# The second tile's attention beside the expert gathers: one step for each part, and the probabilities scaled by VectorE

## What is computed

```python
h = rms_norm(x, mix_norm[i])
q, c_kv, iq, ik, iw, q_mem = jnp.split(h @ a_w_in[j], A_SPLITS, axis=-1)
# dsa_attention, for a block of 128 queries
_, sel = lax.top_k(score, topk)
logits = jnp.einsum('bqhc,bqkc->bhqk', q_lat, c_sel) * (A_HEAD_DIM ** -0.5) + bias
p = jax.nn.softmax(logits, axis=-1)
# memory_attention
logits = jnp.einsum('bqhd,bmhd->bhqm', q, k) * (MEM_HEAD_DIM ** -0.5)
p = jax.nn.softmax(logits, axis=-1)
x = x + jnp.concatenate([seq_out, mem_out], axis=-1) @ w_o[i]
# peer_ffn: 8 retrieval heads of 16 experts = 128 rows of u and of v for each token
act = jax.nn.gelu(jnp.einsum('td,thkd->thk', xt, u[et]))
out = jnp.einsum('thk,thkd->td', act * gt, v[et])
```

## Time and profile before

| | before |
|---|---|
| median of 3 runs | 3037.27 us (3035.47 to 3040.38) |
| profiled execution | 3040.9 us, its span 3039.1 us |
| busy share of the span | PE 82%, DVE 47%, ACT 30%, POOL 23% |
| mean granted TensorE clock | 0.934 of full speed |
| DMA | 1105.17 MB moved, mean 364 GB/s |
| chain that ended last | DMA 43%, PE 40%, DVE 9%, issue 4%, ACT 4% |

### The profile page before, as it was taken

One profiled execution on the slowest core, in us unless ns is written; L12 is line 12 of the kernel. 1 busy time (PEld: TensorE's weight loads), 2 busy tenths in 40 slices (PEclk: granted clock), 3 DMA queues, 4 the chain that ended last, 5 costly groups with the idle time before them and its releaser, 6 DMA issues.

```text
span 3039.1 us, 33538 instructions
## 1 busy us (share of the span) xinstructions
PE 2490.9 (82%) x11846; PEld 1339.6 (44%) x11846; DVE 1422.4 (47%) x3358; ACT 900.5 (30%) x2366; POOL 694.1 (23%) x626
## 2 busy tenths in 40 slices
PE   8999856657999965657899789898987989877776
PEld 8777311113977421212575335463542645422222
DVE  3363100002355201000458766678657786677764
ACT  0131100000122100000235554457434584343433
POOL 4020000001211000000013434324334243444442
PEclk9999887778999988879899999899999999999999
DMA  6337999999434899999739999999999999999997
GB/s 257 143 134 304 415 428 428 427 428 403 174 139 171 368 427 428 428 428 428 313 148 416 381 342 421 422 421 421 422 422 421 416 402 417 421 421 421 420 416 304
DMA packets 123223, 1105.17 MB, mean 364 GB/s; under 512 B 13712, under 2 KB 19120, under 8 KB 23600
## 3 DMA queue, kind: packets, MB, share of 16 engines
q1 hardware_dynamic: 47600, 562.98, 44.5%
q0 software_dynamic: 73728, 536.90, 42.9%
q10 hardware_dynamic: 1728, 3.14, 0.3%
HBM read 1098.78 MB, written 4.19 MB: 363 GB/s over the span
## 4 chain that ended last, share of the span: by engine, by line
DMA 43%; PE 40%; DVE 9%; issue 4%; ACT 4%; POOL 0%; DVEq 0%; SPq 0%; ACTq 0%
DMA wbuf<-in_puv,ar 19%; PE ps L749 16%; PE ps L1541 9%; DMA wbuf<-in_w_expert_up 8%; DMA wbuf<-in_w_expert_down 8%; DMA wbuf<-in_w_expert_gate 5%; PE ps L938 4%; PE ps L1117 3%; DVE wbuf L2376 2%; DMA wbuf<-in_w_mem_kv 2%; PE ps L903 2%; PE ps L753 2%; ACT ar L2439 2%; ACT L2439 1%; PE ps L848 1%
## 5 line engine op out<-in xcount | busy, mean ns | idle before, releaser
L1541 PE MATMUL ps<-wbuf,ar 128*128 128x512 f32 x1960 | 931.8, 614 | 192.7 <-ACT ar L2439 192.6
L2376 DVE CUSTOM_DVE_ANT_0 wbuf<-wbuf,Y 128x1024 f32<-128x1024 f32 x490 | 603.0, 1231 | 314.8 <-DMA wbuf<-in_puv,ar 305.8
L3070 POOL DMA_INDIRECT wbuf<-in_puv,ar x490 | 538.9, 1100 | 828.1 <-PE ps L1541 718.8
L1117 PE MATMUL ps<-wbuf,ar 128*32 128x512 f32 x2944 | 462.1, 765 | 283.3 <-DMA wbuf<-in_w_expert_down 107.2
L1541 PEld LDWEIGHTS ps<-wbuf,ar 128*128 128x128 f32 x1960 | 357.5, 194 | 694.6 <-issue 693.2
L2439 ACT ACTIVATE ar<-ar 128x1 f32<-128x1 f32 (+1 forms) x1051 | 269.5, 256 | 591.1 <-DVE ar L2376 564.9
L749 PE MATMUL ps<-HT,wbuf 128*128 128x128 f32 (+1 forms) x2640 | 410.7, 313 | 7.2 <-DMA wbuf<-in_w_mem_kv 5.9
L749 PEld LDWEIGHTS ps<-HT,wbuf 128*128 128x128 f32 x2640 | 372.7, 193 | 55.8 <-issue 22.1
L1117 PEld LDWEIGHTS ps<-wbuf,ar 128*32 128x32 f32 x2944 | 93.3, 125 | 636.1 <-issue 211.8
L2436 ACT COPY ar<-ps 128x512 f32<-128x512 f32 (+4 forms) x164 | 75.1, 458 | 706.9 <-PE ps L1117 305.3
L3029 POOL TENSOR_TENSOR sm<-sm,co 128x1 f32<-128x1 f32 x18 | 9.9, 552 | 1119.4 <-DVE sm L1576 1119.1
(11 more groups left out here) (203 smaller groups left out, 2071.5 us busy)
## 6 DMA issues: line engine op xcount, KB each, us to landing
wbuf<-in_w_expert_down SPq DMA_DIRECT2D x64, 2048.0 KB, 31.5
wbuf<-in_w_expert_up SPq DMA_DIRECT2D x62, 2048.0 KB, 31.0
wbuf<-in_w_expert_gate SPq DMA_DIRECT2D x58, 2048.0 KB, 30.6
wbuf<-in_w_in SPq DMA_DIRECT2D x22, 2048.0 KB, 9.5
wbuf<-in_peer_w_q SPq DMA_DIRECT2D x14, 2048.0 KB, 11.9
wbuf<-in_w_o SPq DMA_DIRECT2D x6, 2048.0 KB, 11.7
wbuf<-in_b_w_in SPq DMA_DIRECT2D x6, 2048.0 KB, 11.5
wbuf<-in_w_branch_b SPq DMA_DIRECT2D x4, 2048.0 KB, 7.4
```

The lines of the kernel that those rows point to most:

```text
L1117: m = T.e.matmul(ps(jobs[n])[32 * k:32 * k + 32, :], lhs(c, k), v[:, 512 * n:512 * n + 512], start=(c == 0), stop=(c == 7), tile_position= ...
L1541: m = T.e.matmul(acc[n][:, :], DG[:, j % 4, :], rows_of(name)[:, 1024 + 512 * n:1536 + 512 * n], start=(j == 0), stop=(j == 127))
L2376: V.did(V.e.tensor_tensor_reduce(u, u, Y[:, i, :], 1.0, 0.0, ALU.mult, ALU.add, DT[:, i, j:j + 1]), f"dot{l}{i}.{j}")
L3070: G.land(G.e.indirect_dma_start(out=rows_of(name), out_offset=None, in_=I["puv"], in_offset=bass.IndirectOffsetOnAxis(ap=IX[:, i, j:j + 1] ...
```

## The change

The tables by which the steps are taken become maps from a step n to a unit: memory units at n = 2 and 4, head units at n = 19, 21, ..., 29. Each part of a unit has a step of its own, counted from the step of its scores:

| part | engine | before, unit k of the heads at n = | now at n = |
|---|---|---|---|
| scores | TensorE | 19+2k | 19+2k |
| maximum, negation | VectorE | 19+2k | 20+2k |
| Exp | ScalarE | 19+2k | 21+2k |
| reciprocal | VectorE | 21+2k | 22+2k |
| scaling | ScalarE, now VectorE | 21+2k | 22+2k |
| transposes | TensorE | 23+2k | 24+2k |
| copy of the transposed | ScalarE | 23+2k | 24+2k |
| values | TensorE | 27+2k (n = 36 for k = 5) | 26+2k |

The scaling becomes two `tensor_scalar` instructions of VectorE for each of the 8 units (16 in all) in place of 16 ACTIVATE Copy of ScalarE. The tile `tb` has a third buffer, in `cbuf`. GpSimd's masks move from behind the gathers of rows 50, 54, 58 and 62 to rows 52, 56, 60 and 64. `own("ma1.os0")` and `("ma1.os1")` on ScalarE go from n = 30 and 34 to 29 and 33.

```diff
-        MEM_AT = (2, 5, 7, 9, 11)
-        HEADS_AT = (19, 21, 23, 25, 27, 29, 31, 33, 35)
-        NEAR_AT = {42: 0, 44: 1, 50: 2, 54: 3, 58: 4, 62: 5}
+        MEM_AT = {2: 0, 4: 1}
+        HEADS_AT = {19 + 2 * hp: hp for hp in range(6)}
+
+        NEAR_AT = {42: 0, 44: 1, 52: 2, 56: 3, 60: 4, 64: 5}
...
+            def unit_scores(p, u, k):
+                for bi, c0, w, q, kk in u["scores"]:
+                    b = take(f"{p}.s{k}.{bi}")
+                    T.did(mm(b[:, c0:c0 + w], [(q, kk)]), f"{p}.s{k}.{bi}")
+
+            def unit_turned(p, u, k):
+                T.wait_ge(*at[f"{p}.n{k}"])
+                b = take(f"{p}.t{k}.0")
...
+            def unit_values(p, u, k):
+                T.wait_ge(*at[f"{p}.t{k}.0.out"])
...
-                    if n in HEADS_AT or n == 36:
-                        next(heads, None)
+                    if n in HEADS_AT:
+                        unit_scores("ma1", heads[HEADS_AT[n]], HEADS_AT[n])
+                    if n - 7 in HEADS_AT:
+                        unit_values("ma1", heads[HEADS_AT[n - 7]], HEADS_AT[n - 7])
+                    if n - 5 in HEADS_AT:
+                        unit_turned("ma1", heads[HEADS_AT[n - 5]], HEADS_AT[n - 5])
...
+            def unit_max(p, u, k):
+                if k > 2:
+                    V.wait_ge(*at[f"{p}.t{k - 3}.0"])
+                for g in u["soft"]:
+                    bi, c0, w, tab, col0 = g["parts"][0]
+                    V.wait_ge(*at[f"{p}.s{k}.{bi}"])
...
+                ts(u["nm"], u["m"], -1.0, None, ALU.mult, None, f"{p}.nm{k}")
+
+            def unit_root(p, u, k):
+                V.wait_ge(*at[f"{p}.e{k}"])
+                recip(u["den"], u["den"])
+                for n, g in enumerate(u["soft"]):
+                    a0, w = g["cols"]
+                    v = u["tb"][:, a0:a0 + w]
+                    ts(v, v, g["den"], None, ALU.mult, None, *([f"{p}.n{k}"] if n else []))
...
-                    if by_act and 0 <= k - 1 < len(units):
-                        u = units[k - 1]
-                        A.wait_ge(*at[f"{p}.rc{k - 1}"])
-                        for gi, g in enumerate(u["soft"]):
-                            a0, n = g["cols"][0], 128 * len(u["blk"]) // len(u["soft"])
-                            act(u["tb"][:, a0:a0 + n], u["tb"][:, a0:a0 + n], ACT.Copy,
-                                *([f"{p}.n{k - 1}"] if gi + 1 == len(u["soft"]) else []), scale=g["den"])
...
+            def unit_exp(p, u, k):
+                A.wait_ge(*at[f"{p}.nm{k}"])
...
+            def unit_out(p, u, k):
+                job = f"{p}.t{k}.0"
+                A.wait_ge(*at[job])
...
+                    if n - 5 in HEADS_AT:
+                        unit_out("ma1", heads[HEADS_AT[n - 5]], HEADS_AT[n - 5])
+                    if n - 2 in HEADS_AT:
+                        unit_exp("ma1", heads[HEADS_AT[n - 2]], HEADS_AT[n - 2])
```

More of the change, by code:

```diff
@@ L1221, in index_weights @@
                 T.did(T.e.transpose(b[:, 0:64], aIWT[64:128, 128 * i:128 * i + 128], ident[64:128, 64:128]), f"ma{i}.iw")
-            def memory_ready(i):
-                T.wait_ge(*at["mem.v11.out"])
-                T.wait_ge(*at["mem.v10.out"])
-                return attend(f"mm{i}", with_bufs(mem_units(f"mm{i}", 0, half(aQM, i), 1), tb_a[i], pb_a[i]), 2)
             def mix_a():
@@ L1248, in mix_a @@
                 T.did(m, "ma0.rl.0", "ma0.rl.1")
-                memory = memory_ready(0)
+                T.wait_ge(*at["mem.v11.out"])
+                T.wait_ge(*at["mem.v10.out"])
+                memory = attend("mm0", with_bufs(mem_units("mm0", 0, half(aQM, 0), 1), tb_a[0], pb_a[0]), 2)
                 T.wait_ge(*at["ma0.qm.out"])
@@ L1339, in other_half @@
                         T.wait_ge(*at["ma1.qm1.out"])
-                    if n in MEM_AT or n == 12:
-                        next(memory, None)
+                    if n in MEM_AT:
+                        unit_scores("mm1", memory[MEM_AT[n]], MEM_AT[n])
+                    if n - 7 in MEM_AT:
+                        unit_values("mm1", memory[MEM_AT[n - 7]], MEM_AT[n - 7])
+                    if n - 5 in MEM_AT:
+                        unit_turned("mm1", memory[MEM_AT[n - 5]], MEM_AT[n - 5])
                     if n == 19:
@@ L1679, in evac, with attend @@
                     ts(dst, src, scale, None, ALU.mult, None, job + ".out")
-            def attend(p, units, lag, nt, after=None, by_act=False):
+            def attend(p, units, lag, nt, after=None):
                 for k in range(len(units) + lag + 1):
@@ L1719, in attend @@
                         for c in range(0, nb, 4):
-                            if (j + c // 4) % 2 == 0 and not by_act:
+                            if (j + c // 4) % 2 == 0:
                                 job, m = f"{p}.t{j}.{c}", min(4, nb - c)
@@ L2785, in query_chunk @@
                 own(f"p0.w{j}{i}.{k}", half(QT, i)[:, 4 * j + k:4 * j + k + 1])
+            def unit_exp(p, u, k):
+                A.wait_ge(*at[f"{p}.nm{k}"])
+                for n, g in enumerate(u["soft"]):
+                    a0, w = g["cols"]
+                    bi, c0, _, tab, _ = g["parts"][0]
+                    v = u["tb"][:, a0:a0 + w]
+                    act(v, ps(f"{p}.s{k}.{bi}")[:, c0:c0 + w] if tab is None else v, ACT.Exp,
+                        *([f"{p}.s{k}.{bi}.out"] if tab is None else []), *([f"{p}.e{k}"] if n else []),
+                        bias=g["nm"], accum_out=g["den"])
+            def unit_out(p, u, k):
+                job = f"{p}.t{k}.0"
+                A.wait_ge(*at[job])
+                if u["before"] >= 0:
+                    A.wait_ge(*at[f"{p}.pv{u['before']}"])
+                copy(u["pb"], ps(job)[:, :].rearrange("p (k n) -> p k n", k=4), job + ".out")
             def other_half():
-                memory = attend("mm1", with_bufs(mem_units("mm1", 0, half(aQM, 1), 1), tb_a[1], pb_a[1]), 2, 2, by_act=True)
-                heads = attend("ma1", with_bufs(a_units(1), tb_a[1], pb_a[1]), 2, 2, by_act=True)
-                next(memory)
-                next(heads)
+                memory = with_bufs(mem_units("mm1", 0, half(aQM, 1), 1), tb_a[1], pb_a[1])
+                heads = with_bufs(a_units(1), tb_a[1], pb_a[1])
                 for n in range(64):
```

61 lines of the change are left out of this document (41 added, 20 removed).

## The result

The kernel after takes 3019.88 us (median of 4 runs) beside 3037.62 for the kernel before (4 runs): 17.7 us faster, ratio 0.9943, 95% interval 0.9927 to 0.9959. The prediction was 3027.0 with a range from 3022.5 to 3033.5: the direction is right, the size is wrong, and the time lies outside the range. The profiled execution took 3023.03 us, its span is 18.8 us shorter than that of before.

A forecast was written before the change was run, and what follows sets the result against it. It took DMA transfers to bound the kernel, with one 12.4 us hole at the head units; less 2.4 us kept, a gain of 10 us from the median 3037.27 gave 3027, range 3022.5 to 3033.5.

The forecast's parts named there:

- The failed step: Head units' stretch, 1697 to 1800 us: idle DMA share priced the only hole at 12.4 us, the most to be won.
- The reserve: 2.4 us of the 12.4 us hole in the head units' stretch expected to remain after the change.
- The ring and its place: Head units' stretch: GpSimd, TensorE, ScalarE and VectorE wait on each other within one step, making the 12.4 us DMA hole.
- a wait that no row shows as long: The wait that the third `tb` buffer takes away; counted as giving nothing.
- The cover: Head units' stretch: VectorE, scalings included, busy 73.5 to 76.2 of 90.6 us, so the scalings cost nothing beside transfers.
- ScalarE's 6.1 us: Head units: 12 scalings of 0.51 us leave ScalarE, busy 62.6 us; the worth is not added separately.
- part 1: Spreading the head units' parts over steps: waits within one step nearly vanish, with the 12.4 us of idle DMA as path.
- Memory units, third buffer, masks at nothing: Their new places and the third `tb` buffer give nothing; four scalings near 1600 to 1640 cost at most 2.3 us.
- (a): Rival: another ring takes over in the head units' stretch; gain only 3 to 6 us, 3031 to 3034; chance 0.15.
- (b): Rival: gain given back later, or never made since TensorE's plain work made the hole; 3035 to 3038; chance 0.09.
- (c): Rival: slower, VectorE becomes the bound where its busy share passes about 0.95; 3043 to 3046; chance 0.04.
- The leg by GpSimd: Second leg of (c): scalings hold GpSimd's gather issue, 5.6 to 9.1 us if each held one; expected hidden.

The follow-up runs named there:

- Experiment 4: Kernel after with the last stage's row buffers cut from ten to five, four, three and two at rows 24, 48, 72, 96; 3193.41 us in one execution.
- e6: Kernel after with two `tb` buffers in place of three; 3020.75 us, ratio 0.9949.
- experiments 5 to 7: Kernel after with the head units' maximum in the scores' step (3022.02 us), maximum and Exp there (3025.76), or Exp in the maximum's step (3025.01).
- e1: Kernel after with the 16 scalings back on ScalarE, the parts still spread over steps; 3019.44 us, ratio 0.9943.
- e7: Kernel after with each of the 16 scalings followed by three more passes by 1.0 on VectorE; 3030.59 us, ratio 0.9978.
- e2: Kernel before, all parts in its common steps, with the 16 scalings moved from ScalarE to VectorE; 3031.52 us, ratio 0.9985.
- e8: Kernel after with the two memory units as before: common steps, scaled by ScalarE, two `tb` buffers; 3021.56 us, ratio 0.9952.

## Why the prediction was wrong in size and right in its mechanism

1. **The failed step** is the first one: "(0.20 + 0.06 + 0.22 + 0.14) x 20 us = 12.4 us in which the DMA engines had nothing to do", and with it "none beyond these 12.4 can be won". The same rows had the right number in their last column: 421 less 294, 347, 284 and 312 GB/s is 447, times 20 / 421 = 21.2 us, or (421 - 333) / 421 x 103 = 21.5. Experiment 4 shows why the columns differ, the table that time follows the bytes. By the table, bytes worth 22.2 less 1.2 = 21.0 us were made good, and the length from the first gather shrank by 20.1; the first gather came 1.2 us later, which leaves the span's 18.8, and 17.7 is the difference of the medians. The reserve for what stays of the hole was a smaller error (point 3). Since 12.4 was taken for a cap, the range had no room below 3022.5 either.
2. **The ring and its place** hold. One reading in it was off: the view puts VectorE's 13.6 us down to "issue", nothing that it can name, and has a second row for the same maxima that was left out. That row, and TensorE's transposes behind unit 5's scores:

```profile
DVE Y L1701 <- PE ps L753: 7.0, 2, 4.8
...
1768.15 0.66 PE L753 MATMUL ps<-co,Y 128*128 128x128 f32 x4
```

Five of the six maxima waited, 20.6 us. Those of units 2 to 5 began 0.12 to 0.14 us after TensorE's transposes of unit k-2 ended (unit 5: 1768.15 + 0.66, and 1768.94), not after the scores, which end some 0.6 us earlier; it is the wait that two `tb` buffers bring. So "a wait that no row shows as long" was wrong about the third buffer: rows 4 has 2.20 us of it. Scores and transposes stand together in TensorE's step, and it was that step that came late: e6, with two buffers in the spread kernel, can't be told from after.

Waits within one step went (23.0 and 20.6 us to nothing), the row fell from 3.56 to 2.69 us (forecast 2.6 to 2.8), the clock rose from 0.88 to 0.97. That one ring is made of all of them holds too: none of experiments 5 to 7 brought back more than some two fifths of the hole.
3. **The reserve of 2.4 us** for what stays of the hole was generous: 1.2 us by bytes.
4. **VectorE and the scalings.** 12 x 378 + 4 x 367 ns = 6.0 us lie in the range of 5.6 to 9.1 and cost nothing that can be told (e1). The cover was misread, though. "81 to 84%" of 90.6 us became 71.8 of 83 us, 86%, and that mean hides 60 us in which VectorE had none left. The 18.73 of 20 in 1620 to 1640, from which the prediction took that such a load opens no hole, was a VectorE without waits too. It holds at 16 scalings, by the buffers' slack, and fails at 64 (e7).
5. **ScalarE's 6.1 us** were cost inside part 1. Alone they are worth 4.6 us (e2), beside the spread nothing (e1). So the second half of the change isn't needed for its gain, and it used up VectorE's slack.
6. **Memory units, third buffer, masks at nothing**: no cost or gain that can be told (e8 and e6, 2.7 and 1.8 us behind after by the ratios, intervals overlapping); the masks were moved only together with the maximum.
7. **Rivals.** (a) half the gain by another ring: it did not come; TensorE waits 7.7 us for ScalarE, the longest 3.0. (b) nothing given back: the lead of 20 us stays to row 511. (c) slower by VectorE: its mechanism was already there in after, for 60 us and without a price; e7 makes it cost, first in 1740 to 1760, where the prediction would have it. The start was put too high: a VectorE that never waits reads 0.93 to 0.95 here. The leg by GpSimd was seen in one gather at most. The Trainium skill ("SBUF — State Buffer", section "Who interferes with whom") has the engine that issues first hold the shared ports for its whole instruction and the other stand. The stretched VectorE instructions that end with GpSimd's masks agree with that (e7: 1.31 to 2.04 us for 0.17 and 0.35); a scaling that stretches a gather's issue isn't seen. No run isolates the ports.

## What to carry to other kernels

Where a stretch is bound by transfers, price a hole by the missing bytes against a full stretch of the same trace; the busy share showed between a third and three fifths of the missing time in the holes of over 4 us here, and one slice at 1.00 hid 12% of its bytes, in part by small packets. When engines hand work round in a ring, ask for each part one step after it was made: the sum of small distances is worth more than any one of those that were tried, and moving an operation to another engine was worth something only while the ring was closed. A cover of "80% busy" is a mean; look at it in slices as short as the buffers' slack, and look at the engine's waits rather than at its share: one that waits for nothing read 0.94 here.
